# Differential QKV on one Trainium2 core: the rotation's partner rows, swapped by TensorE's product or by four ScalarE copies, and where three weight chunks are asked for

## The reference, cut to what matters

```python
def rope_1d(x, pos):                         # d = 32: one half of a head of 64
    d = x.shape[-1]
    inv = 1.0 / (ROPE_BASE ** (jnp.arange(0, d, 2) / d))
    ang = pos[:, None] * inv[None, :]
    x1, x2 = x[..., : d // 2], x[..., d // 2:]
    return concatenate([x1 * cos(ang) - x2 * sin(ang), x2 * cos(ang) + x1 * sin(ang)], -1)

def rope_2d(x, row, col):
    h = x.shape[-1] // 2
    return concatenate([rope_1d(x[..., :h], row), rope_1d(x[..., h:], col)], -1)

def da_qkv(h, wq, wk, wv, qn, kn, pos):
    q = rms_norm((h @ wq).reshape(B, S, 16, 64), qn)
    k = rms_norm((h @ wk).reshape(B, S, 16, 64), kn)
    v = (h @ wv).reshape(B, S, 8, 128)
    if pos is not None:                      # latent tokens
        q = rope_2d(q, pos[0], pos[1])
        k = rope_2d(k, pos[0], pos[1])
    return q, k, v
```

## Time and profile before

| | us |
|---|---|
| median of 3 runs | 4144.43 |
| lowest and highest run | 4139.06 and 4153.48 |
| the profiled execution | 4142.96 |
| its span in the trace | 4141.2 |
| TensorE busy in it | 3824.2 (92%) |
| VectorE busy | 3237.3 (78%) |
| ScalarE busy | 1728.3 (42%) |
| GpSimd busy | 981.8 (24%) |
| mean of granted TensorE clock over the span | 0.969 of full speed |

### The profile page before, as it was taken

The page is one execution under the profiler, slowest core; times in us unless marked ns, Lnnn a source line. Parts: engine busy times, 40 slices in busy tenths (PEclk is TensorE's granted clock), DMA queues, the critical chain, the costliest instruction groups (busy, mean ns, idle before and its releaser), DMA issues. The chain is left out here.

```text
span 4141.2 us, 55459 instructions
## 1 busy us (share of the span) xinstructions
PE 3824.2 (92%) x20565; PEld 3164.5 (76%) x20565; DVE 3237.3 (78%) x6717; ACT 1728.3 (42%) x2880; POOL 981.8 (24%) x788
## 2 busy tenths in 40 slices
PE   3999988988999999999979898889579999999999
PEld 1554668956899999999944655888579999999998
DVE  2563845986999999999932434469979999999998
ACT  1112622246444444444423444322664444444443
POOL 0000000046333333333300000000653333333332
PEclk8999989999999999999989999999789999999999
DMA  4320012069999999999930000120499999999997
GB/s 186 150 101 31 1 51 91 17 207 289 411 415 411 406 404 405 402 404 404 394 117 22 21 21 21 62 81 22 126 339 416 413 410 407 406 403 402 406 407 303
DMA packets 268124, 1033.68 MB, mean 250 GB/s; under 512 B 147056, under 2 KB 150064, under 8 KB 159920
## 3 DMA queue, kind: packets, MB, share of 16 engines
q0 software_dynamic: 76032, 553.68, 33.3%
q1 hardware_dynamic: 191824, 476.46, 30.4%
HBM read 970.69 MB, written 59.39 MB: 249 GB/s over the span
## 5 line engine op out<-in xcount | busy, mean ns | idle before, releaser
L1480 POOL DMA_INDIRECT gbuf<-in_uv,rows x340 | 514.5, 1513 | 871.0 <-DVE hT L1659 801.2
L1265 POOL TENSOR_SCALAR pqT<-iota,selT 128x128 f32<-128x128 f32 x256 | 200.9, 799 | 1516.9 <-ACT selT L1206 1466.7
L1659 DVE SCALAR_TENSOR_TENSOR hT<-gbuf,act,hT 128x1024 f32<-128x1024 f32 x336 | 416.9, 1282 | 6.0
L1644 DVE SCALAR_TENSOR_TENSOR gbuf<-gbuf,ht 128x1024 f32<-128x1024 f32 x340 | 402.0, 1220 | 0.0
L1480 POOL DMA_INDIRECT xT<-in_uv,rows x172 | 257.5, 1497 | 472.0 <-DVE hT L1659 393.7
L1496 PE MATMUL ps<-h0h,U0h 128*128 128x384 f32 x1024 | 344.2, 336 | 15.8 <-DVE U0l L1618 14.9
L1496 PE MATMUL ps<-h1h,U1h 128*128 128x384 f32 x1024 | 344.5, 336 | 11.8 <-DVE U1l L1618 11.8
L1496 PE MATMUL ps<-h1h,U1l 128*128 128x384 f32 x1024 | 344.2, 336 | 0.0
L1496 PE MATMUL ps<-h0h,U0l 128*128 128x384 f32 x1024 | 344.0, 336 | 0.0
L1496 PE MATMUL ps<-h1l,U1h 128*128 128x384 f32 x1024 | 343.9, 336 | 0.0
L1496 PE MATMUL ps<-h0l,U0h 128*128 128x384 f32 x1024 | 343.6, 336 | 0.0
(11 more groups left out here) (368 smaller groups left out, 9020.9 us busy)
## 6 DMA issues: line engine op xcount, KB each, us to landing
ring<-in_u SPq DMA_DIRECT2D x128, 1024.0 KB, 12.9
ring<-in_v SPq DMA_DIRECT2D x128, 1024.0 KB
ring<-in_wts SPq DMA_DIRECT2D x26, 2048.0 KB, 8.0
gates<-ring SPq DMA_DIRECT2D x32, 1536.0 KB, 8.3
ring<-gates SPq DMA_DIRECT2D x64, 768.0 KB
xT<-in_ada_late SPq DMA_DIRECT2D x24, 1024.0 KB, 5.0
abuf<-in_ada_mid POOLq DMA_DIRECT2D x16, 1024.0 KB, 5.2
gbuf<-in_uv,rows POOLq DMA_INDIRECT x340
```

Of the source, the lines that this page charges most:

```text
L1265: last = pool.tensor_scalar(one2[:, r % 2, t, :], iota[:], selT[:, 1, t0 + t:t0 + t + 1], selT[:, 2, t0 + t:t0 + t + 1], ALU.is_equal, ALU ...
L1480: pool.indirect_dma_start(out=slots[m % GSLOTS], out_offset=None, in_=inp[f"uv{l}"], in_offset=bass.IndirectOffsetOnAxis(ap=rows[:, c:c + ...
L1644: v.scalar_tensor_tensor(u, u, 1.0, ht[:, m // P, :], ALU.mult, ALU.mult, accum_out=act4[:, n % 2, m % 2:m % 2 + 1]).then_inc(sem(n_ + "do ...
L1659: v.scalar_tensor_tensor(y, x, w, y, ALU.mult, ALU.add).then_inc(sem(n_ + "acc"), 1)
```

## The change

The 128 rows of a query or key block are put in another order (`PAIRED`): within each head of 64 rows, the two rows of a pair of the rotation now stand 32 rows apart, so the partners of a quarter of 32 rows are one other quarter. The host reorders the columns of the query and key weights, the gains, the cosine and sine tables, the cached keys, and undoes it for the keys that are put out; the sign is in the sine table. The matmul with `rot_da` is gone. In its place ScalarE copies each quarter of the block to the other quarter's place in `turned`, four copies of 32 x 640 for each of the 16 blocks, and VectorE multiplies `turned` by the sine in place. `values(2)` no longer waits for the last rotation. And SyncE asks for chunks 4, 5 and 6 in `modulation`, each once the adaLN chunk that held its slot has been read, not at the start of `diff_qkv`.

```diff
@@ modulation, SyncE
-                for j in range(SLOTS, N_FIRST):
+                for j in range(SLOTS, J_WQ + 3):
                     load_chunk(sp, ring, j, {j - SLOTS: (sem("ada_mm"), j - SLOTS + 1)})
@@ diff_qkv, SyncE
-                for j in range(J_WQ, J_WV + 2):
+                for j in range(J_WQ + 3, J_WV + 2):
                     load_chunk(sp, ring, j, read)
@@ diff_qkv, TensorE
-                def rotate(i):
-
-                    if i:
-                        pe.wait_ge(sem("rot_v"), 3 * (i - 1) + 1)
-                    product(pe, bank2(6), rot_da, (qT, kT)[i // 8][:, i % 8, 0:T], True, True).then_inc(sem("rot_mm"), 1)
-
                 def values(i):
...
-                    if i == 2:
-                        pe.wait_ge(sem("rot_v"), 3 * 15 + 1)
...
                         squares(i - 1)
                         column_sums(i - 1)
-                    if i >= 2:
-                        rotate(i - 2)
                 squares(15)
                 column_sums(15)
-                rotate(14)
                 values(0)
-                rotate(15)
                 values(1)
@@ diff_qkv, ScalarE
+                def swap(i):
+
+                    act.wait_ge(sem("qk_a"), 2 * i + 1)
+                    if i:
+                        act.wait_ge(sem("rot_v"), 3 * i)
+                    for b in range(4):
+                        half, other = slice(32 * b, 32 * b + 32), slice(32 * (b ^ 1), 32 * (b ^ 1) + 32)
+                        last = act.copy(turned[half, :], (qT, kT)[i // 8][other, i % 8, 0:T])
+                        last.then_inc(sem("swapped"), 1)
+
...
                     act.activation(scr[:, 1 + i % 2, :], bank2(2 * (i % 2)), ACT.Square).then_inc(sem("qk_a"), 1)
+                    if i >= 1:
+                        swap(i - 1)
                     if i == 8:
...
+                swap(15)
                 act.wait_ge(sem("sq_mm"), 16)
@@ diff_qkv, VectorE, rotated(i)
-                    v.wait_ge(sem("rot_mm"), i + 1)
-                    v.tensor_tensor(turned, bank2(6), sin[:, 0:T], ALU.mult).then_inc(r, 1)
+                    v.wait_ge(sem("swapped"), 4 * (i + 1))
+                    v.tensor_tensor(turned, turned, sin[:, 0:T], ALU.mult).then_inc(r, 1)
@@ kernel, on the host
+PAIRED = np.array([64 * c + 32 * half + 16 * pair + j for c in range(2) for pair in range(2) for half in range(2)
+                   for j in range(16)])
...
-    wts += [chunked(a[k][0]) for k in ("da_wq", "da_wk", "da_wv", "da_wo")]
+    wts += [chunked(a[k][0].reshape(D, HDA, P)[:, :, PAIRED].reshape(D, -1)) for k in ("da_wq", "da_wk")]
+    wts += [chunked(a[k][0]) for k in ("da_wv", "da_wo")]
...
+    cos0, sin0 = cos0[PAIRED], sin0[PAIRED] * np.repeat(np.array([-1.0, 1.0, -1.0, 1.0], f), 32)[:, None]
```

More of the change, by code:

```diff
@@ L1848 @@
     gains = np.zeros((P, 16), f)
-    gains[:, 0], gains[:, 1] = np.tile(a["da_q_norm"][0], 2), np.tile(a["da_k_norm"][0], 2)
+    gains[:, 0], gains[:, 1] = np.tile(a["da_q_norm"][0], 2)[PAIRED], np.tile(a["da_k_norm"][0], 2)[PAIRED]
     gains[:, 2] = a["da_subln"][0]
@@ L1890 @@
         "cos_da": cos0, "sin_da": sin0, "cos_mla": cos1, "sin_mla": sin1,
-        "cache_k": a["cache_da_k"][0, 0].reshape(TC, HDA, P).transpose(2, 1, 0),
+        "cache_k": a["cache_da_k"][0, 0].reshape(TC, HDA, P).transpose(2, 1, 0)[PAIRED],
         "cache_v": a["cache_da_v"][0, 0].reshape(TC, HDA * VDA),
@@ L1914 @@
     return (y[TS:].reshape(1, TP, D), y[:TS].reshape(1, TS, D),
-            r["out_da_k"].transpose(2, 1, 0).reshape(1, 1, TP, 2 * HDA, DDA),
+            r["out_da_k"][np.argsort(PAIRED)].transpose(2, 1, 0).reshape(1, 1, TP, 2 * HDA, DDA),
             r["out_da_v"].reshape(1, 1, TP, HDA, VDA),
```

## The result

| | before | changed |
|---|---|---|
| median of the runs, us | 4146.25 (4 runs) | 4115.24 (4 runs) |
| lowest and highest, us | 4139.06 to 4153.48 | 4112.52 to 4117.6 |
| the profiled execution, its span | 4142.96, 4141.2 | 4114.94, 4113.1 |
| TensorE's first query matmul | 102.34 | 84.38 |
| TensorE's first matmul of the attention | 379.99 | 343.98 |

The ratio is 0.9917, with a 95% interval of 0.9902 to 0.9933: the changed kernel is faster, by 31 us between the medians (0.8%). 4108 was forecast, and the range of 4097 to 4119 holds the result. Up to the attention's start the two traces differ by 379.99 - 343.98 = 36.0 us, where 35.7 was forecast; at the end of the span only by 28.1. The experiments are about the parts of the 36.0, about what its cover is worth, and about the 8 us that are missing behind it.

A forecast was written before the change was run, and what follows sets the result against it. The stage was taken to cost its first wait plus TensorE's own work. 18.3 us (start) and 17.4 us (rotation) sum to 35.7 us, taken from 4144.4: 4108 us predicted, range 4097 to 4119, with 0.82 on the forecast.

The forecast's parts named there:

- What bounds the stage: Query/key/value stage: costs its first wait, 32.3 us, plus TensorE's own work; TensorE is never idle from 102.34 us on.
- The start, 18.3 us: Stage start: early chunks let TensorE begin at 84.0 instead of 102.34 us, gaining 18.3 us, ends 16.7 and 18.9.
- the forecast of 84.0: TensorE's first query matmul: activations complete at 83.36 us plus 0.7 for entering the stage.
- The clock at the start: First query block: TensorE still begins at a throttled clock after idling, so the 2.6 us this costs stay.
- The rival of no loss of clock: Stage start: clock already full at 84 us, a further 2.6 us gained, time 4105; chance 0.08.
- The rotation, 17.4 us: TensorE's steps: 16 rotations of 1.09 us leave its path, 17.4 us less, evictions 10.92 us apart.
- ScalarE's copies at nothing: ScalarE's steps: four copies of 0.72 us, 2.9 us a step, fit in a 9.5 us gap and cost nothing.
- The tail: Stage end after the last key eviction: keys' reciprocal ends at 16.3 us, before the next at 18.7; no cover lost.
- The slower rival's price: Copies across quarters take 2.9 us each: step 14.0 us, price 50 us, time 4158; chance 0.02.
- Its loop and its threshold: ScalarE and VectorE: copies wait for the rotation before, rotation for copies; this sets the pace from 2.1 us a copy on.
- The time itself: Whole kernel: median of 4144.4 us less 35.7 gives 4108 predicted; later stages move up as a whole.

The follow-up runs named there:

- the run with this part alone: Kernel before with chunks 4, 5 and 6 asked for in modulation, rotation left on TensorE: 4133.07 us against 4151.65, ratio 0.9961.
- 2 sets free, 3 not: Changed kernel with each block's four copies made twice, or three times, into the same place: 4109.91 us (ratio to before 0.9901), or 4127.4 us (0.9943).
- the run with four sets: Changed kernel with each block's four copies made four times into the same place: 4177.38 us, ratio to before 1.0062.
- the two comparisons: Changed kernel against the kernel before, measured twice, unchanged the second time: 4115.24 against 4146.25 us (0.9917); 4113.97 against 4151.65 us (0.9901).

## Why the prediction held, step by step

- **What bounds the stage.** Right. The first wait and TensorE's own work were all that the stage cost; both shrank, and nothing took their place.
- **The start, 18.3 us.** 102.34 - 84.38 = 18.0 measured, and 18.6 by the run with this part alone. The entry costs 0.3 us and not 0.7; the execution's first stages were 0.7 us later, which took it back. The three early requests did not do that: SyncE issued chunk 3 at 37.82 instead of 37.10, so all of the 0.7 us was there ahead of the first new request. It is scatter of the start (84.4 and 85.1 in the changed kernel's two traces, 84.2 with the early chunks alone). That the forecast of 84.0 came so close is partly luck, two errors of opposite sign.
- **The clock at the start.** Kept at 2.6 us and measured at 2.0: the first block took 95.00 - 84.38 = 10.62 us, the second 8.65. The granted clock was 0.79 in the mean from 60 to 84 us and 0.50 from 75 to 86, where TensorE stood idle and then began; from 88 us on it was 1.00. The rival of no loss of clock (0.08) is out. The rule of the Trainium skill ("TensorE: Matmul & The Clock Gate", section on the clock gate), that the clock is throttled by default and activity releases it, agrees with this trace.
- **The rotation, 17.4 us.** Evictions 10.92 apart, as worked out from the one step of before that had no rotation. The stage lasts 277.65 - 259.6 = 18.05 us less, which is 16 x 1.09 = 17.4 and the 0.6 of the clock.
- **ScalarE's copies at nothing.** Right, with 0.722 us for the 0.72 taken from the straight row, 2.97 us a set, and idle 6.55 us a step for the 6.6 worked out. The nearest row, of another shape and without crossing quarters, was a good price.
- **The tail.** Counted from the last eviction at 256.56, the reciprocal of the keys ended at 268.94 + 4.13 - 256.56 = 16.5 us (16.3 said), the next started at 275.13, 18.6 (18.7 said). No cover was lost:

```profile
268.94 4.13 DVE L419 RECIPROCAL scr_da<-scr_da 16x640 f32<-16x640 f32 x1
275.13 0.66 DVE L421 RECIPROCAL rsq<-ps 128x80 f32<-128x80 f32 x1 [2.06 <-PE ps L304]
```

- **The slower rival's price.** Its loop and its threshold are shown (2 sets free, 3 not). Its pitch of 14.0 us for copies of 2.9 us (4 x 2.9 + 2.5 is 14.1) is near that of the run with four sets (14.56, with three more semaphores), but 50 us was too little: 65 at the attention's start, and 58 to 65 between the medians (each against the kernel before beside it), since TensorE also waits for ScalarE's work behind the copies, and these waits bring the clock down. That sits beyond the forecast and changed nothing in it.
- **The time itself.** 4108 was some 7 us too low against 4115.24, and the mechanism isn't at fault: the gain of 35.7 us stands against 36.0 in the traces up to the attention, and 31.0 and 37.7 between the medians of the two comparisons. The term that was off is the base that the gain was taken from. 4144.43 was the median of three runs; three later sets of 11, 16 and 7 runs of the same kernel have medians of 4150.44, 4151.65 and 4150.51, some 6 to 7 us higher. Less 35.7 that gives 4114.7 to 4116.0, where the changed kernel's medians are 4115.24 and 4113.97. The trace that the rows come from was short as well, 3761.2 us behind the attention's start against 3765.4 to 3778.1 in the nine others. That the rest of the program moves as a whole holds in the mean, but its attention, late gates and last experts scatter by 2.5, 4 and 7.5 us between two executions of one program. The range held because it allowed for a median 8 us off, worked out from the spread of the runs.

## What to carry to other kernels

Where a stage waits for a load that is asked for at its own start, look at the DMA share of the stages ahead: if it is zero and the slot is free, asking there costs one issue and gives back the part of the wait that is the load's alone (here 18.0 of 32.3 us; the rest was the norm's). When work is moved to an idle engine, price the loop it joins (here copies, rotation, copies) and not that engine's free time alone; the room in the loop was 8.3 us where the engine's own would have been 9.5. Compare two traces stage by stage, and take a second trace of the same kernel before a difference far from the change is given a cause.

## What the runs showed of the hardware

ScalarE's copy from one group of 32 partitions to another costs 722 ns for 640 float32 columns, as much as a straight activation of 128 partitions (721). One idle time of 4.84 us in an otherwise full TensorE brought the granted clock to 0.50, where it stayed for the next 8 us of work. And equal programs differ in late stages: the kernel before waited 1.0 us for its gates' stores in one execution and 5.0 in another, in a stage that was 4 us longer there.
